# Gathering an expert row as two half rows, through two rings of slots

## The reference, cut to what matters

```python
s = jnp.einsum('thpd,phkd->pthk', qh, sub_keys)
sv, si = lax.top_k(s, PK_TOPK)
...
best, pos = lax.top_k(cand, PK_TOPK)
eidx = jnp.take_along_axis(cidx, pos, axis=-1)
gate = jax.nn.softmax(best, axis=-1)
...
act = jax.nn.gelu(jnp.einsum('td,thkd->thk', hb, u_tab[eb]))
return jnp.einsum('thk,thkd->td', gb * act, v_tab[eb])
```

## Time and profile before

| | |
|---|---|
| median of 3 runs | 4477.78 us (4476.44 to 4484.85) |
| span of the profiled execution | 4473.8 us |
| first gather issued | 1276.5 us |
| accumulator of the last tile read (L874) | 4465.2 us |
| PE, DVE, ACT, POOL busy over the span | 84%, 58%, 24%, 29% |
| data moved by the gathers | 1208 MB |

### The profile page before, as it was taken

The page is one execution under the profiler, slowest core; times in us unless marked ns, Lnnn a source line. Parts: engine busy times, 40 slices in busy tenths (PEclk is TensorE's granted clock), DMA queues, the critical chain, the costliest instruction groups (busy, mean ns, idle before and its releaser), DMA issues.

```text
span 4473.8 us, 40368 instructions
## 1 busy us (share of the span) xinstructions
PE 3754.3 (84%) x10642; PEld 1830.8 (41%) x10642; DVE 2602.6 (58%) x6424; ACT 1077.7 (24%) x2678; POOL 1282.6 (29%) x1174
## 2 busy tenths in 40 slices
PE   8999999999967788877878887787888887887777
PEld 3766766555433333333333333333333333333222
DVE  4544545233257676666566656666666666666555
ACT  3444543000012222222222222212222222222211
POOL 0000000000014334444343434443443343334433
PEclk9999999999989999999999999999999999999999
DMA  4000002211559999999999998999999999999998
GB/s 167 21 27 28 17 8 89 97 66 52 193 213 355 388 354 400 368 395 370 391 374 379 397 387 362 394 398 366 382 394 378 376 393 394 382 367 398 421 422 360
DMA packets 187700, 1310.84 MB, mean 293 GB/s; under 512 B 24082, under 2 KB 25618, under 8 KB 36274
## 3 DMA queue, kind: packets, MB, share of 16 engines
q0 software_dynamic: 165888, 1208.03, 66.9%
q1 hardware_dynamic: 21684, 101.33, 5.9%
HBM read 1299.28 MB, written 10.00 MB: 293 GB/s over the span
## 4 chain that ended last, share of the span: by engine, by line
PE 56%; DMA 23%; issue 9%; DVE 7%; ACT 3%; POOL 1%; DVEq 0%; POOLq 0%; SPq 0%; ACTq 0%
PE ps L530 23%; DMA arena<-in_uv,arena 22%; PE ps L1097 8%; PE ps L449 8%; PE ps L490 5%; PE ps L473 3%; DVE arena L843 2%; ACT arena L625 2%; PE ps L1141 1%; PE ps L1091 1%; PE ps L1158 1%; POOL arena L415 1%; DVE arena L779 1%; DVE arena L715 1%; PE ps L504 1%
## 5 line engine op out<-in xcount | busy, mean ns | idle before, releaser
L530 PE MATMUL ps<-arena 128*128 128x512 f32 x4608 | 2226.2, 633 | 618.0 <-ACT arena L625 617.6
L843 DVE CUSTOM_DVE_ANT_0 arena<-arena 128x1024 f32<-128x1024 f32 x1152 | 1407.9, 1224 | 767.2 <-DMA arena<-in_uv,arena 703.6
L415 POOL DMA_INDIRECT arena<-in_uv,arena x1152 | 1276.4, 1108 | 1919.9 <-PE ps L530 1760.0
L530 PEld LDWEIGHTS ps<-arena 128*128 128x128 f32 x4608 | 888.1, 200 | 1907.7 <-ACT arena L625 953.2
L625 ACT ACTIVATE arena<-ident,arena 128x128 f32<-128x128 f32 x1152 | 398.3, 393 | 1200.9 <-DVE arena L832 1200.8
L1097 PE MATMUL ps<-arena 128*128 128x384 f32 x1152 | 388.5, 494 | 15.1 <-issue 13.2
L449 PE MATMUL ps<-arena 128*128 128x384 f32 x1152 | 373.7, 487 | 2.5 <-DMA arena<-in_w_mg 2.5
L406 POOL IOTA arena<- 128x16 f32 x1 | 0.1, 145 | 1244.6 <-DMA x_scratch<-arena 1244.6
L1097 PEld LDWEIGHTS ps<-arena 128*128 128x128 f32 x1152 | 218.0, 193 | 160.3 <-issue 23.0
L449 PEld LDWEIGHTS ps<-arena 128*128 128x128 f32 x1152 | 218.2, 190 | 159.7 <-issue 6.0
L619 ACT ACTIVATE arena<-arena 128x2 f32<-128x2 f32 x576 | 116.2, 202 | 663.2 <-DVE arena L843 662.7
(11 more groups left out here) (200 smaller groups left out, 2463.8 us busy)
## 6 DMA issues: line engine op xcount, KB each, us to landing
arena<-in_w_mod SPq DMA_DIRECT2D x12, 2048.0 KB, 23.3
arena<-in_uv,arena POOLq DMA_INDIRECT x1152, 9.9
arena<-in_w_in SPq DMA_DIRECT2D x28, 512.0 KB, 3.3
arena<-in_w_mg SPq DMA_DIRECT2D x8, 1536.0 KB, 6.5
arena<-x_scratch SPq DMA_DIRECT2D x18, 512.0 KB, 11.9
arena<-in_w_q SPq DMA_DIRECT2D x4, 2048.0 KB, 20.9
arena<-in_xT SPq DMA_DIRECT2D x4, 1152.0 KB, 13.4
arena<-in_x_tok SPq DMA_DIRECT2D x9, 512.0 KB, 4.6
```

Source lines behind the costliest of these rows:

```text
L415: nc.gpsimd.indirect_dma_start(out=RG[:, s, :], out_offset=None, in_=uv, in_offset=bass.IndirectOffsetOnAxis(ap=IDXS[:, par_, s:s + 1], ax ...
L530: mm = nc.tensor.matmul(PS[:, n, :], DG[:, s, :], RG[:, s, D + n * 512:D + (n + 1) * 512], start=False, stop=False, skip_group_check=True)
L843: ins = v.tensor_tensor_reduce(RG[:, s, 0:D], RG[:, s, 0:D], H2C, 1.0, 0.0, ALU.mult, ALU.add, PRE[:, s:s + 1])
```

## The change

A row of `uv` is now addressed as two half rows (`uv_rows`, 32768 rows of 4 KB). A slot's u half goes by one indirect DMA into the ring `UR`, its v half by another into the ring `VR`; both have 8 slots of half the size, in the same memory. POOL issues, for slot n, first the u half of slot n and then the v half of slot n - 4 (LAG = 4). The u half's place is free once DVE's dots of the group that held it are done (`dots`); the v half's place once PE has used it (`v_used`). DVE waits for `u_in`, PE now waits for `v_in` and `diag_ready`. ACT, which was covered by the single ring, now waits itself for `v_used` before it rewrites a diagonal matrix. DVE writes two sets of indices a round, 2e and 2e + 1, into four buffers in place of two, and POOL's loop body holds four rounds in place of two.

```diff
+LAG = 4
+IDX_BUFS = 4
...
-    RG = AR[:, A_RING:A_B].rearrange("p (s c) -> p s c", s=RING)
+    UR = AR[:, A_RING:A_RING + RING * D].rearrange("p (s c) -> p s c", s=RING)
+    VR = AR[:, A_RING + RING * D:A_B].rearrange("p (s c) -> p s c", s=RING)
+    uv_rows = uv.rearrange("e (h d) -> (e h) d", h=2)
...
-        def fetch(r, par_, first=False):
-            pool.wait_ge(idx_r, r + 1)
+        def fetch_u(r, b, s, first=False):
+            if s == 0:
+                pool.wait_ge(idx_r, r + 1)
+            if not first:
+                wait_alone(pool, dots, r * (RING // GRP) + (s // GRP + 1 - RING // GRP))
+            nc.gpsimd.indirect_dma_start(
+                out=UR[:, s, :], out_offset=None, in_=uv_rows,
+                in_offset=bass.IndirectOffsetOnAxis(ap=IDXU[:, b, s:s + 1], axis=0),
+            ).then_inc(u_in[s], 16)
+
+        def fetch_v(r, b, s, first=False):
+            if not first:
+                wait_alone(pool, v_used, r * RING + (s + 1 - RING))
+            nc.gpsimd.indirect_dma_start(
+                out=VR[:, s, :], out_offset=None, in_=uv_rows,
+                in_offset=bass.IndirectOffsetOnAxis(ap=IDXV[:, b, s:s + 1], axis=0),
+            ).then_inc(v_in[s], 16)
+
+        def fetch(r, b, before, first=False, first_v=False):
             for s in range(RING):
-                if not first:
-                    wait_alone(pool, v_used, r * RING + (s + 1 - RING))
-                nc.gpsimd.indirect_dma_start(
-                    out=RG[:, s, :], out_offset=None, in_=uv,
-                    in_offset=bass.IndirectOffsetOnAxis(ap=IDXS[:, par_, s:s + 1], axis=0),
-                ).then_inc(gathered[s], 16)
+                fetch_u(r, b, s, first)
+                if s < LAG:
+                    if not first:
+                        fetch_v(before, (b - 1) % IDX_BUFS, s + RING - LAG, first_v)
+                else:
+                    fetch_v(r, b, s - LAG, first)
...
+                    pe.wait_ge(v_in[s], (t * ROUNDS + i * RPP + q) * 16 + 16)
                     pe.wait_ge(diag_r, n0)
                     for n in range(2):
-                        mm = nc.tensor.matmul(PS[:, n, :], DG[:, s, :], RG[:, s, D + n * 512:D + (n + 1) * 512],
+                        mm = nc.tensor.matmul(PS[:, n, :], DG[:, s, :], VR[:, s, n * 512:(n + 1) * 512],
...
                     act.wait_ge(coef_r, n + 1)
+                    if not (first and q == 0):
+                        act.wait_ge(v_used, n * GRP + (GRP - RING))
...
+        def round_index(b, at):
+            v.tensor_scalar(IDXU[:, b, :], EIDX[:, at], 2, None, ALU.mult)
+            v.tensor_scalar(IDXV[:, b, :], EIDX[:, at], 2, 1, ALU.mult, ALU.add).then_inc(idx_r, 1)
...
-                        dve.wait_ge(gathered[s], (t * ROUNDS + i * RPP + q) * 16 + 16)
-                        ins = v.tensor_tensor_reduce(RG[:, s, 0:D], RG[:, s, 0:D], H2C, 1.0, 0.0, ALU.mult,
+                        dve.wait_ge(u_in[s], (t * ROUNDS + i * RPP + q) * 16 + 16)
+                        ins = v.tensor_tensor_reduce(UR[:, s, :], UR[:, s, :], H2C, 1.0, 0.0, ALU.mult,
```

More of the change, by code:

```diff
@@ L294, in build @@
     EIDX, GATE = sm(2 * P, dt=U32), sm(2 * P)
-    IDXS = sm(2, RING, dt=U32)
+    IDXU, IDXV = sm(IDX_BUFS, RING, dt=U32), sm(IDX_BUFS, RING, dt=U32)
     iota = sm(TOPK)
@@ L310, in build @@
     pair_done, idx_r = sem("pair_done"), sem("round_index_ready")
-    gathered = [sem(f"gathered{n}") for n in range(RING)]
+    u_in, v_in = [sem(f"u_in{n}") for n in range(RING)], [sem(f"v_in{n}") for n in range(RING)]
     dots, gel_r, coef_r, diag_r, v_used = (sem(x) for x in ("dots", "gelu_ready", "coef_ready", "diag_ready",
@@ L407, in stage_b_pool @@
                        allow_small_or_imprecise_dtypes=True).then_inc(it_r, 1)
-        def fetch(r, par_, first=False):
-            pool.wait_ge(idx_r, r + 1)
-            for s in range(RING):
-                if not first:
-                    wait_alone(pool, v_used, r * RING + (s + 1 - RING))
-                nc.gpsimd.indirect_dma_start(
-                    out=RG[:, s, :], out_offset=None, in_=uv,
-                    in_offset=bass.IndirectOffsetOnAxis(ap=IDXS[:, par_, s:s + 1], axis=0),
-                ).then_inc(gathered[s], 16)
[L420 to L424, removed]
+        def fetch_u(r, b, s, first=False):
[15 more added lines that the diff above has]
+        def fetch(r, b, before, first=False, first_v=False):
+            for s in range(RING):
+                fetch_u(r, b, s, first)
[4 more added lines that the diff above has]
+                    fetch_v(r, b, s - LAG, first)
+        fetch(0, 0, 0, first=True)
+        fetch(1, 1, 0, first_v=True)
+        fetch(2, 2, 1)
+        fetch(3, 3, 2)
+        with pool.Fori(1, TILES * ROUNDS // IDX_BUFS) as i:
+            for b in range(IDX_BUFS):
+                fetch(i * IDX_BUFS + b, b, i * IDX_BUFS + (b - 1))
+        for s in range(RING - LAG, RING):
+            fetch_v(TILES * ROUNDS - 1, IDX_BUFS - 1, s)
     def stage_b_pe(pe):
@@ L611, in two_pairs_between, with rounds @@
                     9: lambda: scores_out(tn, i + 1), 10: lambda: gates(tn, i), 15: lambda: gates(tn, i + 1)}
-        def rounds(t, i, between):
+        def rounds(t, i, between, first=False):
             for q in range(RPP):
@@ L645, in stage_b_act @@
             gates(0, i)
-        rounds(0, 0, two_pairs_between(0, 2))
+        rounds(0, 0, two_pairs_between(0, 2), first=True)
         rounds(0, 1, front_between(1))
@@ L853, in rounds @@
                 if not last or q < 2:
-                    v.tensor_copy(IDXS[:, q % 2, :], EIDX[:, bass.ds(i * RPP * RING + (q + 2) * RING, RING)])\
-                        .then_inc(idx_r, 1)
+                    round_index((q + 2) % IDX_BUFS, bass.ds(i * RPP * RING + (q + 2) * RING, RING))
             coef(t, i, *todo)
@@ L937, in stage_b_dve @@
         for q in range(2):
-            v.tensor_copy(IDXS[:, q, :], EIDX[:, q * RING:(q + 1) * RING]).then_inc(idx_r, 1)
+            round_index(q, slice(q * RING, (q + 1) * RING))
         v.tensor_copy(H2C, H2N).then_inc(c_shift, 1)
```

## The result

The kernel after took 4550.36 us (median of 4 runs, 4548.64 to 4557.72), the kernel before 4478.21 us beside it (4 runs, 4476.44 to 4484.85): ratio 1.0162, 95% interval 1.0147 to 1.0176. It is 72 us slower, where 22 were forecast. In a later set of runs it took 4549.93 us again (ratio 1.0161). In yet another it took 4926.53 us with the kernel before unchanged at 4479.24; the experiments come to that. What follows compares the profiled execution of 4546.9 us span with that of before, 4473.8.

What follows compares the result with a forecast made beforehand. POOL's issues were to replace the transfer and PE's stops as the bound: 3198 us of issues and holds, plus 33, minus 16 and 4, made a 3211 us stage, 22 us more, so 4500 us in all; range 4310 to 4670 us.

Steps and rivals of the forecast that it cites:

- Free issues: POOL's 2304 half-row issues when nothing stops them: 1.243 us each, 2.486 us a slot, 2864 us in all.
- Holds by dots: POOL's issues starting within a DVE dot are held until 0.81 us behind its end: 0.29 us a slot.
- Stops before `keys_best`: DVE's idle time there grows some 5 us, 33 times; POOL mostly covers it, charged 1 us each, 33 us.
- the lag is not covered: Rival: POOL has no places left during DVE's longer stops before `keys_best`; 165 us lost, about 4640 us; chance 0.09.
- Gains taken off: POOL goes on over DVE's gaps at tile ends, 16 us off; PE follows the last v landings, 4 us off.
- By tile: Last tile slows from 324 to 355 us, tiles 1 to 7 stay, tile 0 may gain.
- in step: Rival: POOL's issues fall in step with DVE's dots; a slot costs 2.56 to 2.64 us, 4332 us; chance 0.32.
- The signs named beforehand: In the profile: POOL near 85% busy, idle mostly "issue", mean issue above 1.0 us, last tile longer, PE awaiting `v` landings.

Runs made afterwards that it cites:

- e1: The kernel after with the copy of the token's row that the dot reads moved from SBUF into PSUM: 4391.41 us, ratio 0.9810.
- run 20: No follow-up run: words of "let POOL run 20 us", the time the prediction let POOL go on issuing from the last dot before a stop.
- e14: The kernel after with the u half issued two slots ahead of the v half in place of four: 4533.07 us, ratio 1.0138.
- e4: The kernel after with only the first 512 of a v row's 1024 elements gathered: 4597.28 us, ratio 1.0266.

## Why the prediction was wrong in size, point by point

The sign, the bound and the mechanism of the holds held; the forecast of +22 us was a third of the +72 measured. What failed is the term for the stops before `keys_best`, 33 us where POOL's waits are 86, and the 20 us of gains that were taken off and the end that was left out. The stage was to take 3211 us and took 3260, from the first issue at 1278.24 to the reading of the accumulator at 4538.27; the first issue came 1.7 us later. By the terms of the sum:

- **Free issues**, 2864 us: 2860. Two issues a slot at 1.243 us is what bounds the kernel.
- **Holds by dots**, 0.29 us a slot, 334 us: 303, or 0.263 a slot. The mechanism is as read: an issue that starts 0.1 us into a dot takes 1.92 us on average, at 0.5 us 1.53, at 0.9 us 1.13, and at 1.1 us 0.94, which is "until the dot's end and 0.81 more". e1 shows it from the other side: with one of the dot's operands in PSUM an issue takes 0.94 us wherever in the dot it starts. The rule of the Trainium skill (SBUF — State Buffer, Who interferes with whom) that I set beside it is borne out so far. The other half of how I put it, that a dot is blocked by an issue which came first, does not show: 938 of the 1152 dots start within an issue, and they take 1.22 us like the rest, none above 1.30, and start no later behind their landing. Only the issue pays.
- **Stops before `keys_best`**, 1 us each, 33 us: this step failed most. All waits above the free pace are 86 us, of which the waits for the dots are 84.7 - 31 x 0.30 = 75. POOL's and DVE's timelines at one such stop:

```profile
3076.09 0.94 POOL L419 DMA_INDIRECT arena<-in_uv,arena  x1 [0.30 <-issue]
3077.33 0.94 POOL L428 DMA_INDIRECT arena<-in_uv,arena  x1 [0.30 <-issue]
3081.65 0.94 POOL L419 DMA_INDIRECT arena<-in_uv,arena  x1 [3.38 <-DVE arena L878]
```

```profile
3067.45 0.16 DVE L862 TENSOR_TENSOR arena<-arena 128x2 f32<-128x2 f32 x1 [6.19 <-ACT arena L647]
3067.52 1.23 DVE L878 CUSTOM_DVE_ANT_0 arena<-arena 128x1024 f32<-128x1024 f32 x1
...
3077.42 0.87 DVE L745 MAX8 arena<-arena 128x8 f32<-128x128 f32 x4 [8.66 <-ACT arena L626]
3078.43 1.22 DVE L878 CUSTOM_DVE_ANT_0 arena<-arena 128x1024 f32<-128x1024 f32 x1
...
3079.66 1.22 DVE L878 CUSTOM_DVE_ANT_0 arena<-arena 128x1024 f32<-128x1024 f32 x1
```

  DVE stands 6.19 us, does one dot, and stands another 8.66 us. POOL goes on, reaches the u half whose place the next dots must free, and waits 3.38 us. 18 waits of 3.2 to 6.1 us, all but one near 3.4 from tile 2 on, make up 68 of the 84.7. I had let POOL run 20 us, 8 u halves, from the last dot before the stop. But the ring isn't empty then. Counted by the starts of L419 and the ends of L878, 3 of its 8 places are taken at the steady pace (the dots follow the issues by the landing, 6.3 us), 5 when the second stop begins at 3068.75, and 8 at 3077.4. I had also looked for a longer stop at `keys_best`, and that did not come (289.4 us, before 285.9). The lag's delay makes a stop of its own one step earlier, before L862, for the gelu that ACT does behind the queries: 206.9 us in 38 waits, where the kernel before has 53.7. That is the wait that the prediction did not have. The rival "the lag is not covered" had the right place and too high a price: by e14 it is some 17 to 31 us, not 165.
- **Gains taken off**, 16 us at the tiles' ends and 4 at the end. Neither was there to take: the sum was built from POOL's issues alone, and the gaps of the kernel before were no part of it. What a model of one engine does not contain cannot be subtracted from it. The end was short by more: from the last issue to the reading of the accumulator 4538.27 - 4527.49 = 10.8 us pass (landing, then PE's last slots), which 1152 x 2.776 left out.

```profile
4526.47 1.02 POOL L428 DMA_INDIRECT arena<-in_uv,arena  x1 [0.30 <-issue]
```

```profile
4538.27 1.22 DVE L908 TENSOR_TENSOR arena<-ps,arena 128x1024 f32<-128x1024 f32 x1 [8.60 <-PE ps L558]
```

Together: -4 for the issues, -31 for the holds, 86 - 33 for the waits, 16 for the tiles' ends and 4 + 11 for the end of the stage make +49, the 3260 - 3211.

**By tile.** The last was to take 355 us; it took 338: the rival "in step" came true there and only there. Its issues beside a quiet stretch of dots:

```profile
4502.19 0.94 POOL L419 DMA_INDIRECT arena<-in_uv,arena  x1 [0.30 <-issue]
4503.44 1.00 POOL L428 DMA_INDIRECT arena<-in_uv,arena  x1 [0.30 <-issue]
4504.74 0.94 POOL L419 DMA_INDIRECT arena<-in_uv,arena  x1 [0.30 <-issue]
```

```profile
4502.40 1.23 DVE L878 CUSTOM_DVE_ANT_0 arena<-arena 128x1024 f32<-128x1024 f32 x1 [1.25 <-DMA arena<-in_uv,arena]
```

A slot takes 4504.74 - 4502.19 = 2.55 us, the dot meets only the end of one issue and the start of the next, and the tile's holds are 12 us, where tiles 0 to 7 have 31 to 41 each. There the DMA engines are the other limit, and they move what the 4 KB rows had shown, against 422 before:

```profile
DMA packets 7863, 28.66 MB, mean 409 GB/s; under 512 B 871, under 2 KB 871, under 8 KB 7861
```

In tiles 2 to 7 the pace is 2.82 us a slot; that the retrieval's steps put the dots out of step there is argued from their absence in the last tile, not tested. Tile 0 did not gain, 392 us against 389.

**The signs named beforehand.** POOL's busy share was to come near 85% and came to 76%; idle mostly "issue", mean issue above 1.0 us, PE waiting for `v` landings, an unchanged 0.94 us: seen. The last tile got longer and fell from 410 to 402 GB/s, as named, but its DMA share was to fall and did not (1.01, before 0.99). In tiles 2 to 7 the share stayed near the top at fewer GB/s (0.99 at 375), which I had said would mean rows slower than 409 GB/s. That reading was wrong: e1 moves 398 GB/s in its tiles 2 to 7 with the same rows, at a share of 1.01, so a share of 0.99 doesn't say that the transfer is at its best rate. Nor does a share above 1 come from packets counted whole at a window's edges alone, as I had put it: e1's window is 2046 us long.

## What to carry to other kernels

Where a gather is issued by POOL at 1.24 us apiece, count issues before bytes: splitting each in two put 2.49 us of issuing against 2.49 us of transfer, and all that holds the issuing engine came on top. Look first at what holds it (here a dot with both operands in SBUF) and take that away; only then did the two rings pay here, and a lag of 2 was better than one of 4. In a sum built on one engine, add each wait of that engine and the path from its last instruction to the end, and subtract nothing that was never in it. For a ring that is to cover a stop, count how many of its places are taken when the stop begins.

## What the runs showed of the hardware beyond that

- An indirect DMA of 128 rows costs POOL 0.94 us and 0.30 us before the next one, with rows of 8 KB, 4 KB and, for the v rows of e4, 2 KB (shortest 0.932, 0.932 and 0.942 us).
- The hold is one-sided and sharp: 761 issues of the kernel after start within a dot, more than 0.11 us before its end, and nine in ten of them end 0.807 to 0.814 us behind the dot's end; a dot that starts within an issue is not delayed.
- Fewer bytes made a kernel slower: e4, by 47 us, with 107 us more of holds and 56 us less of waits.
- The same program with 2304 gathers took 4550 us in two sets of runs and 4927 in a third, always beside the kernel before within 4476 to 4480. A change that reads +1.6% in one set reads +10% in another, so kernels to be compared must run in one set. At the high level the traces also lack about half of their semaphore records. Which of the two levels is the usual one stays open.
